# Projections of a recurrence's stage: from three matmuls per tile pair to two, with a PSUM bank for each half unit

## The reference, cut to what matters

```python
u = _rms_norm(h, g_pre[i])
cols = u @ w_in[i]
qa, ka, va, za = (a_cols[..., j * A_WIDTH:(j + 1) * A_WIDTH] ... for j in range(4))
y_a = _moba_attention(qa, ka, va, rel_bias) * jax.nn.silu(za)
y_b, z_b = _rwkv7_time_mix(b_cols, ...)
merged = sigmoid(gate_a) * (y_a @ p_a[i]) + sigmoid(gate_b) * (y_b * silu(z_b) @ p_b[i])
```

## Time and profile before

| | us |
|---|---|
| three timed executions | 887.79, 878.88, 884.30 |
| their median | 884.30 |
| the profiled execution, whole | 881.41 |
| its span, first to last instruction | 879.4 |
| PE busy in the span | 863.8 |
| DVE busy | 670.4 |
| ACT busy | 482.9 |

### The profile page before, as it was taken

The page is one execution under the profiler, slowest core; times in us unless marked ns, Lnnn a source line. Parts: engine busy times, 40 slices in busy tenths (PEclk is TensorE's granted clock), DMA queues, the critical chain, the costliest instruction groups (busy, mean ns, idle before and its releaser), DMA issues. The chain is left out here.

```text
span 879.4 us, 19235 instructions
## 1 busy us (share of the span) xinstructions
PE 863.8 (98%) x7612; PEld 787.8 (90%) x7612; DVE 670.4 (76%) x999; ACT 482.9 (55%) x779; POOL 119.5 (14%) x136
## 2 busy tenths in 40 slices
PE   7999999999999999999999999999999999999998
PEld 7999888888889988898888888899999888899998
DVE  6996887777767876768877767786996687748775
ACT  5774565555445576655555554459523654434453
POOL 2003300000122000050000007630017010000110
PEclk9999999999999999999999999999999999999999
DMA  9542555554556533155555445674443353234541
GB/s 343 191 170 104 173 181 187 187 188 146 190 197 225 193 113 113 64 192 191 191 190 189 165 163 183 216 272 145 145 146 121 121 135 83 98 135 145 166 170 48
DMA packets 23410, 144.50 MB, mean 164 GB/s; under 512 B 2968, under 2 KB 3224, under 8 KB 9648
## 3 DMA queue, kind: packets, MB, share of 16 engines
q1 hardware_dynamic: 22032, 140.26, 46.4%
q0 software_dynamic: 1168, 3.23, 1.7%
q10 hardware_dynamic: 144, 0.06, 0.0%
HBM read 142.47 MB, written 1.06 MB: 163 GB/s over the span
## 5 line engine op out<-in xcount | busy, mean ns | idle before, releaser
L2091 DVE TENSOR_TENSOR lo<-raw,hi 128x1024 fp32r<-128x1024 f32 (+1 forms) x210 | 244.1, 1204 | 12.2 <-ACT hi L1492 9.0
L583 PE MATMUL ps<-X,hi 128*128 128x512 f32 x704 | 244.7, 392 | 0.0
L582 PE MATMUL ps<-X,lo 128*128 128x256 f32 x704 | 197.1, 280 | 0.8 <-DVE X L2106 0.6
L576 PE MATMUL ps<-X,hi 128*128 128x256 f32 x600 | 174.2, 290 | 0.2
L577 PE MATMUL ps<-X,hi 128*128 128x256 f32 x600 | 169.7, 283 | 0.0
L578 PE MATMUL ps<-X,lo 128*128 128x256 f32 x600 | 169.7, 283 | 0.0
L583 PEld LDWEIGHTS ps<-X,hi 128*128 128x128 f32 x704 | 131.9, 187 | 29.4
L582 PEld LDWEIGHTS ps<-X,lo 128*128 128x128 f32 x704 | 132.6, 188 | 2.5 <-issue 1.9
L1492 ACT ACTIVATE hi<-raw 128x1024 fp32r<-128x1024 f32 (+1 forms) x109 | 107.7, 988 | 28.4 <-DMA raw<-in_wide 15.0
L583 PE MATMUL ps<-H,hi 128*128 128x512 f32 x352 | 122.1, 392 | 0.0
L576 PEld LDWEIGHTS ps<-X,hi 128*128 128x128 f32 x600 | 114.9, 191 | 4.8 <-issue 3.3
(11 more groups left out here) (400 smaller groups left out, 1445.1 us busy)
## 6 DMA issues: line engine op xcount, KB each, us to landing
raw<-in_wide SPq DMA_DIRECT2D x106, 1024.0 KB, 4.9
raw<-in_down SPq DMA_DIRECT2D x32, 704.0 KB, 4.0
BI<-bias_table POOLq DMA_DIRECT2D x16, 128.0 KB, 4.9
raw<-in_wide SPq DMA_DIRECT2D x3, 512.0 KB, 8.9
X<-in_x SPq DMA_DIRECT2D x1, 1024.0 KB, 13.4
WG<-in_group SPq DMA_DIRECT2D x1, 768.0 KB, 17.2
out<-X SPq DMA_DIRECT2D x3, 256.0 KB, 2.4
cmask<-in_masks POOLq DMA_DIRECT2D x1, 544.0 KB, 6.5
```

Of the source, the lines that this page charges most:

```text
L576: nc.tensor.matmul(dst, wh, xh, start=first, stop=False, skip_group_check=True)
L582: nc.tensor.matmul(bank[:, 0:T], wl, x[:, 0, :], start=first, stop=False, skip_group_check=True)
L583: return nc.tensor.matmul(bank, wh, x, start=False, stop=last, skip_group_check=True)
L2091: nc.vector.tensor_tensor(lo[:, s, a:b], raw[:, s, a:b], hi[:, s, a:b].bitcast(F32), ALU.subtract).then_inc(lo_ready, 1)
```

## The change

Queries, keys, ZA and the merging gates (14 of the 16 units) are multiplied with `wide_product`. Each half unit then fills a bank of its own, so each of these units takes two bank uses instead of one. The half's result is read in two stages: ACT copies the right half of the bank into the result's SBUF tile (`lower_terms`), then DVE adds the left half to it and multiplies by the factor, for each half unit. Two semaphores are new: `tile_done` (PE has finished a first half unit) and `tile_lower` (ACT has copied). The values' units (115, 116) stay as they were.

```diff
@@ first_group
+    g += max(0, min(u - U_QA, U_VA - U_QA)) + max(0, min(u - U_ZA, U_PA - U_ZA))
@@ tables
+        def wide_fill(u):
+            return U_QA <= u < U_VA or U_ZA <= u < U_PA
+
+        def tile_count(u, half):
+            n = u - U_QA if u < U_VA else u - U_ZA + U_VA - U_QA
+            return 2 * n + half + 1
+
+        def tile_made(u, half):
+            for u0, tiles_ in ((U_GATE, SGT), (U_ZA, ZA), (U_KA, KA), (U_QA, QA)):
+                if u >= u0:
+                    return tiles_[:, 2 * (u - u0) + half, :]
@@ PE, fill
-                gate = U_GATE <= u < U_PA or U_QA <= u < U_VA or U_ZA <= u < U_GATE
-                if gate:
+                if wide_fill(u):
                     if first:
-                        if half == 0:
-                            bank_free(g)
+                        bank_free(g + half)
                         half_ready(u, half)
                     for k in ks:
                         c = slice((half * KD + k) * P, (half * KD + k + 1) * P)
-                        last = product(PROJ[g % 2][:, half * T:(half + 1) * T], hi[:, u % 4, c], lo[:, u % 4, c],
-                                       XH[:, k, :], XL[:, k, :], half == 0 and k == 0, k == KD - 1)
+                        last = wide_product(PROJ[(g + half) % 2], hi[:, u % 4, c], lo[:, u % 4, c], X2[:, :, k, :],
+                                            k == 0, k == KD - 1)
+                    if half == 0 and part != 0:
+                        last.then_inc(tile_done, 1)
@@ PE, mlog
-                pe.wait_ge(evac_done, first_group(U_KA + 1) + 1)
+                pe.wait_ge(evac_done, first_group(U_KA + 1) + 2)
@@ ACT
+            def lower_terms(u, half):
+                if u == U_QA and half == 0:
+                    act.wait_ge(hats_done, 1)
+                if half == 0:
+                    act.wait_ge(tile_done, tile_count(u, 0) // 2 + 1)
+                else:
+                    act.wait_ge(unit_done, u + 1)
+                bank = PROJ[(first_group(u) + half) % 2]
+                nc.scalar.activation(tile_made(u, half), bank[:, T:2 * T], ACT.Copy).then_inc(tile_lower, 1)
+
             def fill(u, half, part=None):
+                if wide_fill(u) and part != 0:
+                    lower_terms(u, half)
                 if not U_QA < u < U_PA:
                     split_half(u + AHEAD, half)
@@ DVE, fill
-                if u < U_PA and half == 0 or part == 0:
+                if U_VA <= u < U_ZA and half == 0 or part == 0:
                     return
-                if u < U_KA:
-                    take(u, QA[:, 2 * (u - U_QA):2 * (u - U_QA) + 2, :], SCALE)
-                elif u < U_VA:
-                    take(u, KA[:, 2 * (u - U_KA):2 * (u - U_KA) + 2, :])
+                if wide_fill(u):
+                    dve.wait_ge(tile_lower, tile_count(u, half))
+                    t = tile_made(u, half)
+                    link(nc.vector.tensor_tensor(t, t, PROJ[(g + half) % 2][:, 0:T], ALU.add))
+                    nc.vector.scalar_tensor_tensor(t, t, SCALE if u < U_KA else 1.0, RS[:, 1, :], ALU.mult,
+                                                   ALU.mult).then_inc(evac_done, 1)
+                    if u >= U_ZA and half:
+                        dve.wait_ge(evac_done, g + 2)
+                        dve.sem_inc(za_in if u < U_GATE else gates_in, 1)
...
-                elif u < U_GATE:
-                    j = u - U_ZA
-                    take(u, ZA[:, 2 * j:2 * j + 2, :])
-                    dve.wait_ge(evac_done, g + 1)
-                    dve.sem_inc(za_in, 1)
-                elif u < U_PA:
-                    j = u - U_GATE
-                    take(u, SGT[:, 2 * j:2 * j + 2, :])
-                    dve.wait_ge(evac_done, g + 1)
-                    dve.sem_inc(gates_in, 1)
```

More of the change, by code:

```diff
@@ L281, in program @@
         lower_in = sem("lower_in")
+        tile_done, tile_lower = sem("tile_done"), sem("tile_lower")
         x_part = sem("x_part")
```

## The result

The changed kernel takes 889.3 us (median of 16 executions, 885.62 to 895.34) against 884.3 for the kernel before: a ratio of 1.0072, 95% interval 1.0052 to 1.0092. Run once more beside the kernels of a later experiment it gave 1.0071 (1.0045 to 1.0098). So it is about 0.7%, some 6 us, slower: a difference that repeats, and inside the 1% that the prediction called "same". The profiled execution of the changed kernel is 887.26 us, its span 885.2.

What follows compares the result with a forecast made beforehand. PE was taken to pace the stage, with DVE close behind in its first two thirds. The terms -3.1 + 2.4 + 4.4 = +3.7 us on a level of 883.1 gave 887 us; range 880 to 896.

Steps and rivals of the forecast that it cites:

- Part 1: PE in the 14 changed units: 224 steps of two matmuls instead of three, 0.014 us less each, gain 3.1 us.
- Part 2: Stage start: PE waits before unit 112 until DVE has read the first half of unit 111, 2.4 us lost.
- Part 3: Added DVE and ACT work delays PE at later places in the crowded part, 4.4 us lost; bounds 0 and 11.7.
- `level_n` of level 1: DVE's copy ends late for PE's block after three more evictions of halves, 0.6 us lost.
- ZA: Units 117, 118: ACT's copy stands ahead of the SiLU, with no slack; 0.6 us lost at the first, 0.9 at the second.
- first `level_y` of the second group: PE's block near 717.93: DVE has both halves of 118 and the first of 119 behind it, 0.95 us lost.
- unit 121's bank: First half of unit 121 waits for the bank of 120's first half, read only after `mnorm`; 0.55 us lost.
- `grams(1, 2)`: This block already waits for ACT, which now has one more copy ahead; 0.35 us lost.
- A: DVE and ACT hide the new work in idle time: 882.4 us, down to 880.0; chance 0.17.
- B: DVE and ACT become the bound in the crowded part: +11.0, 894.1 us; chance 0.19.
- C: The clock falls once or twice at the waits near 638.6 or 706.48: 888.5 to 890.2 us; chance 0.12.
- D: Weight loads pace PE, so the change takes out 26.9 us, leaving about 860; chance 0.02.

Runs made afterwards that it cites:

- e5: Against e1, VectorE reads only each bank's left half, once, and ScalarE copies nothing in the other 12 changed units; 882.1 us, ratio 0.9988 to the kernel before.
- e1: Against the changed kernel, the queries (units 111, 112) go back to three 256-column matmuls, one bank a unit; 886.9 us, ratio 1.0034 to the kernel before.
- e2: Against the changed kernel, evictions of unit 111's halves go ahead of the splits of unit 113 on VectorE; 888.2 us, ratio 1.0041 to the kernel before.
- r_after: The changed kernel run once more, nothing changed; 887.9 us, ratio 1.0071 to the kernel before.
- e6: Against e1, ScalarE's 24 copies are removed and VectorE's addition takes a tile already in SBUF; 885.1 us, ratio 1.0016 to the kernel before.
- e3: Against the changed kernel, nine unused matmuls stand on TensorE ahead of the wait for unit 112's bank; 888.9 us, ratio 1.0037 to the kernel before.
- r_busy: The kernel of e3 run once more, nothing changed; 887.9 us, ratio 1.0046 to the kernel before.
- e4: Against the changed kernel, the 28 ScalarE copies and 28 VectorE additions are removed, leaving one read per bank; 883.3 us, ratio 1.0005 to the kernel before.
- g_early: Against the changed kernel, the output gates' eight units go back; queries, keys and gate stay changed; 886.3 us, ratio 1.0041 to the kernel before.
- g_gates: Against the changed kernel, queries, keys and gate go back; only output gates' units 119 to 126 stay changed; 885.8 us, ratio 1.0025 to the kernel before.
- g_keys: Against the changed kernel, all but the two units of the keys (113, 114) go back; 882.3 us, ratio 0.9989 to the kernel before.

## Why the prediction was right or wrong

**The forecast as a whole.** 887 us was right in sign and class, and short by some 2 us: +3.7 forecast, +5.85 in the stage. The part that failed is the decision to leave the clock out of the sum: the fall behind the first wait cost 1.7 us. The time of 887 against 889.3 says less than the stage does, for its level, 883.1, was 1.2 us under the median of the kernel before, and the medians differ by 5.0 us.

**Part 1** was right in kind, and mis-sized: 3.1 forecast, 2.5 by the step (0.349 instead of 0.346), 1.6 for twelve units when all else is taken away (e5). The feed-forward net's steps stand in one long row, and here a run of them is 8 or 16 long and broken by the recurrence; whether that is the reason was not tried.

**Part 2** was right to 0.1 us: 2.4 forecast, 2.29 measured, at the place and for the releaser that were named. e1 takes it away with its unit, e2 with its order.

**Part 3** was right in sum, 4.4 forecast against 3.8 in the waits (4.4 if the pause before the change is not counted as one) and 4.17 between e1 and e5. It was mixed in its places, so the closeness of the sum is partly luck:

- `level_n` of level 1, 0.6 forecast: the view has no wait there, the starts have 0.23 us (r_after has one of 0.5 us at a later level).
- ZA, 0.6 and 0.9: the stage grew by 0.57 and 0.60 us there. That ACT's copy is the main reason, as forecast, e6 shows.
- first `level_y` of the second group, 0.95: 0.53.
- unit 121's bank, 0.55: 0.94; the `level_n` behind it, 0.45: 0.41. Together the stage grew by 0.58 us there, since the pause of before stood in the same place. The slack of 0.08 us at that `level_n` was read behind the pause.
- `grams(1, 2)`, 0.35: 1.4 instead of 1.1 at the turned tile and 0.2 more behind it.
- "None added after 767": wrong, 0.59 us for DVE's WU (L2768) at 780. Nor does PE stream without a gap after 800 us: the kernel before idles for 0.62 us at 844.

**Rivals.** A fell: e5 shows the -1.6 us that hidden work would have left, and the changed kernel is 7.5 us of stage above it. B fell: PE waits once each at a `level_y` and a `level_n` (the lines of L2744 and L2756 above), not at most of the ten levels. C came true in addition to the forecast, and not in its place: I had given it 0.12 because 1.00 us of idle time had not done it. The new wait is 2.29 us, more than twice that row, and it was my own number. e3 and r_busy show that it is this idle time that does it. D fell, with steps of 0.349; but that the busy time of the weight loads follows the columns does not hold either, for at equal columns it fell from 146.7 to 134.2 us in the stage.

**Busy times.** DVE +12.3 (forecast 15 to 17) and ACT +9.1 (about 11): an add and a multiplication take 0.79 us from one half's start to the next (641.50 to 642.29 in the timeline above), where I had 0.87 to 0.90, and the page counts the time in which two instructions of an engine overlap only once. Why ACT's is 1.5 us under its 28 copies was not looked into. PE's idle time from 640 to 767 rose by 5.5 us (forecast 5 to 8).

## What to carry to other kernels

When an instruction is saved on the busiest engine by reading its result in one more stage elsewhere, price the chain from the last matmul to the released bank, place by place, and not the engines' busy shares: 2.5 us won here cost 2.3 us at one queue position and about 4 us in short waits. A wait that is new on TensorE can have a second price: here 1.84 to 2.29 us of unbroken idle time behind short matmuls were followed by a lower granted clock in four profiles of four, at 1.7 us each. Look for it and add it to the sum. Measure in the stage, between two blocks that both kernels have, when executions differ by more than the effect, and compare starts of blocks as well as listed waits.

## What was not expected of the hardware

**The fall of the clock is the same size each time.** It cost 1.7 us in each of six places that were summed, in stretches of 2 us (behind the wait in changed: 0.74, 0.50, 0.91; r_after: 0.52, 0.63; e4: 0.88, 0.50, 0.77; g_early: 0.54, 0.60; e3 at 762: 0.59, 0.56; before at 846: 0.51, 0.64). It does not follow from the idle time alone: e1 and the changed kernel idle for the same 1.9 us around 760 as e3 does, without a fall. The Trainium skill (page "TensorE: Matmul & The Clock Gate", section "Part 1: The HAM clock gate (the "warmup" mystery)") holds that activity keeps the clock up and that the watch on it runs free of the kernel. e3 against r_busy agrees with that, if it means that the same idle time can be caught in one execution and missed in another; no run here tries it further.

**Steps can be 2% slower at a full clock.** In seven of the fourteen profiled executions a long run of two-matmul steps that the change does not touch is 0.3533 us apart in place of 0.3467: from 402 to 565 us in e1 to e3, g_gates, g_early and g_keys, from 150 to 400 us in e5, with a granted clock of 1.00. Groups by line from 410 to 560 us, before and then e1:

```profile
L583 PE MATMUL ps<-X,hi 128*128 128x512 f32 x298 | 103.4, 394 | 0.0
L582 PE MATMUL ps<-X,lo 128*128 128x256 f32 x297 | 82.3, 277 | 0.0
```

```profile
L599 PE MATMUL ps<-X,hi 128*128 128x512 f32 x301 | 106.4, 399 | 0.0
L598 PE MATMUL ps<-X,lo 128*128 128x256 f32 x300 | 84.3, 281 | 0.0
```

That is 3.0 us over 163 us, most of the 4.4 us by which e1 reaches the stage later than the kernel before (the rest is a fall of the clock in its first 16 us). Its cause was not tried and stays open; it belongs to executions, not to the change (e3 has it, and r_busy, the same kernel, has not), and is one reason why single times of this kernel spread by 9 us.
